# First FFN of a conditioned decoder layer: its first four hidden chunks computed from x*(1+scale), with the shift added afterwards as a bias, and eight conditioning blocks loaded in other stages

## The reference

```python
mod = silu(c) @ w_ada + b_ada              # (B, 9*1024)
sh1, sc1, gt1, sh2, sc2, gt2, sh3, sc3, gt3 = split(mod, 9)
h = x * (1 + sc1) + sh1
x = layer_norm(ALPHA * x + 0.5 * gt1 * swiglu(h, ffn1_w_in, ffn1_w_out))
h = x * (1 + sc2) + sh2
m = hybrid_mixer(h, ...)                   # conv branch and pooling branch, gated, one output projection
x = layer_norm(ALPHA * x + gt2 * m)
h = x * (1 + sc3) + sh3
x = layer_norm(ALPHA * x + 0.5 * gt3 * swiglu(h, ffn2_w_in, ffn2_w_out))
# swiglu: gate, up = split(h @ w_in, 2); (silu(gate) * up) @ w_out, hidden width 2816
```

## Time and profile before

| | |
|---|---|
| median of 3 runs | 1577.0 us |
| the profiled execution, its own time | 1571.29 us |
| its span on the slowest core (core 5) | 1569.7 us |
| spans of the 8 cores | 1556.7 to 1569.7 us |
| PE busy | 1479.4 us (94%), 9258 matmuls |
| PEld (weight loads, beside PE) | 856.3 us (55%) |
| DVE / ACT / POOL busy | 44% / 30% / 9% |
| chain of work that ended last | PE 84%, DMA 9%, DVE 3%, ACT 2%, issue 2% |
| DMA queue of POOL (q0), share of 16 engines | 48.6% |
| DMA queue of SP (q1), share of 16 engines | 20.9% |

### The profile page before, as it was taken

The page is one execution under the profiler, slowest core; times in us unless marked ns, Lnnn a source line. Parts: engine busy times, 40 slices in busy tenths (PEclk is TensorE's granted clock), DMA queues, the critical chain, the costliest instruction groups (busy, mean ns, idle before and its releaser), DMA issues.

```text
span 1569.7 us, 24460 instructions; the slowest of 8 cores (1556.7 to 1569.7 us)
## 1 busy us (share of the span) xinstructions
PE 1479.4 (94%) x9258; PEld 856.3 (55%) x9258; DVE 688.6 (44%) x935; ACT 472.9 (30%) x688; POOL 133.9 (9%) x253
## 2 busy tenths in 40 slices
PE   0799999999899999999999999999999999999995
PEld 0466666544344457765664564445666665444454
DVE  1223323565222465972377687237431134441255
ACT  0011112253112264672127456113531111421124
POOL 2011111000110000000000000000000010000000
PEclk9999999999999999999999999999999999999998
DMA  9989999869977868635386964457586465584522
GB/s 185 180 141 196 196 215 186 167 110 190 186 137 145 144 155 232 182 72 131 55 174 143 243 182 105 97 104 154 118 178 131 74 132 97 111 170 84 113 70 99
DMA packets 94980, 227.03 MB, mean 145 GB/s; under 512 B 10848, under 2 KB 36192, under 8 KB 94688
## 3 DMA queue, kind: packets, MB, share of 16 engines
q0 software_dynamic: 37136, 124.11, 48.6%
q1 hardware_dynamic: 57728, 101.36, 20.9%
HBM read 299.64 MB, written 40.11 MB: 216 GB/s over the span
## 4 chain that ended last, share of the span: by engine, by line
PE 84%; DMA 9%; DVE 3%; ACT 2%; issue 2%; SPq 0%; DVEq 0%; ACTq 0%; POOL 0%; POOLq 0%
PE ps L354 78%; PE ps L769 4%; DMA VS<-pool_w 3%; DMA ring<-ffn_w_in 2%; DMA VS<-R 2%; DMA XS<-tp_dr 1%; DMA ring<-w_ada 1%; DVE VB L322 1%; PE ps L418 1%; DVE hA L319 1%; ACT L315 1%; ACT scr L315 0%; PE ps L544 0%; ACT rstd_sb L315 0%; ACT VB L315 0%
## 5 line engine op out<-in xcount | busy, mean ns | idle before, releaser
L354 PE MATMUL ps<-hA,ring 128*128 128x348 bf16 x3072 | 467.2, 312 | 8.1 <-DMA ring<-ffn_w_in 3.6
L354 PE MATMUL ps<-hB,ring 128*128 128x512 bf16 x2048 | 450.9, 380 | 10.0 <-DVE mpv L513 5.3
L354 PE MATMUL ps<-R,ring 128*128 128x348 bf16 (+3 forms) x2378 | 398.7, 327 | 0.0
L354 PEld LDWEIGHTS ps<-hA,ring 128*128 128x128 bf16 x3072 | 298.1, 97 | 170.1 <-issue 9.6
L354 PEld LDWEIGHTS ps<-hB,ring 128*128 128x128 bf16 x2048 | 200.0, 98 | 250.6 <-issue 15.7
L315 ACT ACTIVATE scr<-ps 128x1044 f32<-128x1044 f32 (+1 forms) x136 | 140.3, 1032 | 633.8 <-PE ps L354 629.8
L354 PEld LDWEIGHTS ps<-R,ring 128*128 128x128 bf16 x2378 | 229.3, 97 | 163.1 <-issue 0.2
L319 DVE TENSOR_TENSOR R<-ps,scr 128x1024 bf16<-128x1024 f32 (+2 forms) x112 | 128.8, 1156 | 429.9 <-PE ps L354 387.0
L315 ACT ACTIVATE scr<-VB 128x1044 f32<-128x1044 f32 (+3 forms) x56 | 51.5, 919 | 296.8 <-DVE VB L322 121.1
L322 DVE SCALAR_TENSOR_TENSOR VB<-ps,modT,XS 128x1024 f32<-128x1024 f32 (+4 forms) x56 | 55.1, 983 | 97.1 <-PE ps L354 94.1
L303 POOL DMA_DIRECT2D ring<-ffn_w_in x88 | 46.6, 531 | 470.8 <-PE ps L354 440.2
(11 more groups left out here) (121 smaller groups left out, 802.7 us busy)
## 6 DMA issues: line engine op xcount, KB each, us to landing
ring<-ffn_w_in POOLq DMA_DIRECT2D x88, 512.0 KB, 10.0
ring<-w_in POOLq DMA_DIRECT2D x40, 512.0 KB, 7.5
ring<-w_ada POOLq DMA_DIRECT2D x36, 512.0 KB, 15.8
ring<-ffn_w_out POOLq DMA_DIRECT2D x48, 352.0 KB, 6.3
XS<-tp_dr SPq DMA_DIRECT2D x48, 288.0 KB, 4.5
tp_dr<-VS SPq DMA_DIRECT2D x32, 288.0 KB, 15.5
XS<-x_b SPq DMA_DIRECT2D x16, 512.0 KB, 9.8
VS<-R SPq DMA_DIRECT2D x128, 64.0 KB, 5.6
```

The lines of the kernel that those rows point to most:

```text
L354: ins = e.matmul(o, lt, rt[:, c0:c0 + n], start=(i == 0), stop=(i == nk - 1))
```

## The change

- In `setup` x of group A comes in three column tiles (1024 rows of 1392 B each) in place of four pairs of chunks, and only `ada_block(2)` and `(3)` are run, which now hold all of scale 1 (the host no longer reorders the columns). From each tile `hpre` = x*(1+scale) is made as soon as it is there, on VectorE (6 chunks) and ScalarE (2 chunks).
- `ffn_in_early` runs blocks 0 and 1 of the first FFN (j = 0 to 3) on `hpre`; block 0 tile by tile. The sums are copied from PSUM to eight spare places (`pre`).
- Then `ada_block(0)` and `(1)` (shift 1), `consts_early`, and `shift_bias`: 64 matmuls of 17 columns multiply the shift with the same weight blocks 0 and 1. `h_shifted` makes the usual `hA`, and the main loop starts at block 2. `finish_early` adds the bias to the saved sums in the hooks of j = 4 to 7.
- The ada blocks move: 4 to 8 at j = 6, 9, ..., 18; 9 to 11 at oc = 1, 3, 5 of the first FFN out of A; 12 to 15 in the mixer of A, after oc = 1, 3, 5, 7 of the second `gated` call; 16 and 17 in the mixer of B, after oc = 1 and 5 there.

```diff
@@ -419,8 +419,7 @@
                                        start=(k == 0), stop=(k == KC - 1))
                 return ins
             S.add("pe", fn, reads=[ring[:, s, :], cT[:, :, :]], writes=[ps[:, bank, 0:68]])
-            pieces = [(2 * i, 2, 0), (8 + 2 * i, 2, 34)] if i < 4 else [(4 * i, 4, 0)]
-            for idx, n, o in pieces:
+            for idx, n, o in [(4 * i, 4, 0)]:
                 src = ps[:, bank, o:o + n * 17].rearrange("p (m t) -> p m t", t=17)
                 dst = modT[:, idx:idx + n, :]
                 bb = baT[:, idx:idx + n].unsqueeze(2).to_broadcast([128, n, 17])
@@ -449,9 +448,10 @@
         def setup():
             dma("sp", "s_c", [(cin[:, :, :], c_all.rearrange("p (c t) -> p c t", t=17))], [], [cin[:, :, :]])
             dma("sp", "s_p", [(baT[:, :], ba_d[:, :]), (pT[:, :], pv_d[:, :])], [], [baT[:, :], pT[:, :]])
-            for i in range(4):
-                o = VB[:, 2 * i * GA.W:(2 * i + 2) * GA.W].rearrange("p (c n) -> p c n", c=2)
-                dma("sp", "s_x%d" % i, [(o, x_d["a"][2 * i:2 * i + 2].rearrange("c p n -> p c n"))], [], [o])
+            for i, (c0, n) in enumerate(GA.tiles):
+                o = XV[:, :, c0:c0 + n]
+                dma("sp", "s_x%d" % i, [(o, x_d["a"][:, :, c0:c0 + n].rearrange("c p n -> p c n"))], [],
+                    [chunk(VB, GA, c)[:, c0:c0 + n] for c in range(KC)])
             mset(ones_bf[:, :], 1.0 / D)
             mset(epsT[:, 0:1], EPS)
             mset(epsT[:, 1:2], EPS_DN)
@@ -460,11 +460,73 @@
             for m, f in gate_f.items():
                 b = baT[:, m * 8:(m + 1) * 8]
                 S.add("dve", lambda e, b=b, f=f: e.tensor_scalar_mul(out=b, in0=b, scalar1=f), reads=[b], writes=[b])
-            for i in range(4):
-                ada_block(i)
-                for c in (2 * i, 2 * i + 1):
-                    h_main(GA, c, chunk(VB, GA, c), 0, "dve")
-                    h_samp(GA, c, chunk(VB, GA, c), 0)
+            mset(hpre[:, :, NP + SW:GA.W], 0.0)
+            ada_block(2)
+            ada_block(3)
+            for c0, n in GA.tiles:
+                n = min(n, NP - c0)
+                for c in range(KC):
+                    o, i_ = hp(c)[:, c0:c0 + n], chunk(VB, GA, c)[:, c0:c0 + n]
+                    if c % 3 == 2:
+                        act(o, i_, AF.Identity, scale=modp(1, c))
+                    else:
+                        S.add("dve", lambda e, o=o, i_=i_, s=modp(1, c): e.tensor_scalar_mul(out=o, in0=i_, scalar1=s),
+                              reads=[i_, modp(1, c)], writes=[o])
+            xs_ = XV[:, :, NP:NP + SW]
+            tt(hpre[:, :, NP:NP + SW], xs_, modT[:, 8:16, 1:17], ALU.mult)
+
+        XV = VB[:, :].rearrange("p (c n) -> p c n", n=GA.W)
+        hpre = R[:, 14616:14616 + 8352].rearrange("p (c n) -> p c n", n=GA.W)
+        shb = cin[:, :, :].rearrange("p c t -> p (c t)").bitcast(BF16)[:, 0:KC * 17].rearrange("p (c t) -> p c t", t=17)
+        pre = [XS[:, i, :] for i in range(3)] + [mean_sb[:, :], rstd_sb[:, :]] + [
+            R[:, 8352 + 2088 * i:8352 + 2088 * i + 2088].bitcast(F32) for i in range(3)]
+
+        def hp(c):
+            return hpre[:, c, :]
+
+        def ffn_in_early(blk):
+            s = wblock(ffn_in_w[0][blk])
+            v = sl(s, KC, 512)
+            for jj in range(2):
+                j = 2 * blk + jj
+                groups = [[t] for t in range(GA.nt)] if blk == 0 else [list(range(GA.nt))]
+                for ts_ in groups:
+                    for b in range(2):
+                        o = b * 256 + jj * 128
+                        bk = bank(b, GA)
+                        mm([bk[t] for t in ts_], lambda k, o=o: v[:, k, o:o + 128], hp, KC)
+                act(P3(pre[2 * j], GA), pb(0, GA), AF.Copy)
+                cpy(P3(pre[2 * j + 1], GA), pb(1, GA))
+            return v
+
+        def shift_bias(vs):
+            cpy(shb, modT[:, 0:8, :])
+            for j in range(4):
+                for b in range(2):
+                    i = 2 * j + b
+                    o = b * 256 + (j % 2) * 128
+                    out = ps[:, 6, i * 17:(i + 1) * 17]
+                    mm([(out, 0, 17)], lambda k, o=o, j=j: vs[j // 2][:, k, o:o + 128], lambda k: shb[:, k, :], KC)
+            p6 = ps[:, 6, 0:136].rearrange("p (i t) -> p i t", t=17)
+            cpy(csb[:, :, :], p6[:, :, 1:17])
+            cpy(mpv[:, :, 0:1], p6[:, :, 0:1])
+
+        def h_shifted():
+            for c in range(KC):
+                h_main(GA, c, chunk(VB, GA, c), 0, "act" if c % 3 == 2 else "dve")
+            t = ctx[:, :, :]
+            tt(t, XV[:, :, NP:NP + SW], modT[:, 8:16, 1:17], ALU.mult)
+            tt(h_t["a"][:, :, NP:NP + SW], t, modT[:, 0:8, 1:17], ALU.add)
+
+        def finish_early(j):
+            a, b = pre[2 * j], pre[2 * j + 1]
+            for i, v in ((2 * j, a), (2 * j + 1, b)):
+                tt(v[:, NP:NP + SW], v[:, NP:NP + SW], csb[:, i, :], ALU.add)
+            z = scr[j % 2]
+            act(z[:, 0:NP], a[:, 0:NP], AF.Silu, bias=mpv[:, 2 * j, 0:1])
+            act(z[:, NP:GA.W], a[:, NP:GA.W], AF.Silu)
+            stt(hid(GA, j)[:, 0:NP], b[:, 0:NP], mpv[:, 2 * j + 1, 0:1], z[:, 0:NP], ALU.add, ALU.mult)
+            tt(hid(GA, j)[:, NP:GA.W], b[:, NP:GA.W], z[:, NP:GA.W], ALU.mult)
 
         def consts_early():
             dma("pool", "s_w", [(mask[:, :, :], mask_d.rearrange("p (c q) -> p c q", q=4)),
@@ -550,9 +612,9 @@
         def shift_state():
             dma("sp", "sshift", [(ncs_d[:, :, :], sconv[:, 1:30, :]), (nps_d[:, :, :], spool[:, 1:15, :])], [], [])
 
-        def ffn_in(g, f, hook):
+        def ffn_in(g, f, hook, b0=0):
             hh = h_t[g.name]
-            for blk in range(FC // 2):
+            for blk in range(b0, FC // 2):
                 s = wblock(ffn_in_w[f][blk])
                 v = sl(s, KC, 512)
                 for jj in range(2):
@@ -701,7 +763,7 @@
         def wpk(h):
             return ("wp_dr", 0, 1, 8 * h, 8 * h + 8)
 
-        def mixer(g, x1name, x1src):
+        def mixer(g, x1name, x1src, late_ada):
             first = g is GA
             hh = h_t[g.name]
             hrhs = lambda k: hh[:, k, :]
@@ -937,6 +999,8 @@
                         else:
                             stt(P3(z, g), P3(z, g), 1.0, pb(1, g), ALU.add, ALU.mult)
                             tt(merged(oc), z, m1, ALU.add)
+                            if oc % 2 and oc in late_ada:
+                                ada_block(late_ada[oc])
                         bg.step(2 if oc else 3)
 
             gated(8, lambda h: wblock(wp_dr[h], key=[wpk(h)]), pooled, UORD, True, gb_w)
@@ -1008,27 +1072,32 @@
         setup()
 
         def hook_f1in_a(j):
-            if j == 1:
-                consts_early()
-            if j >= 2 and j % 2 == 0 and j <= 12:
-                ada_block(4 + (j - 2) // 2)
-            if j in (15, 19):
-                ada_block(10 + (j - 15) // 4)
+            if j < 8:
+                finish_early(j - 4)
+            if j in (6, 9, 12, 15, 18):
+                ada_block(4 + (j - 6) // 3)
             if j >= 6:
                 build_toep(2 * (j - 6))
                 build_toep(2 * (j - 6) + 1)
             if j == 20:
                 consts_late()
 
-        ffn_in(GA, 0, hook_f1in_a)
+        v0 = ffn_in_early(0)
+        v1 = ffn_in_early(1)
+        ada_block(0)
+        ada_block(1)
+        consts_early()
+        shift_bias([v0, v1])
+        h_shifted()
+        ffn_in(GA, 0, hook_f1in_a, 2)
         h0b = gen_h0b()
 
         def hook_f1out_a(oc):
             next(h0b, None)
             if oc == 0:
                 next(h0b, None)
-            if oc in (1, 4):
-                ada_block(12 + oc // 4)
+            if oc in (1, 3, 5):
+                ada_block(9 + oc // 2)
 
         ffn_out(GA, 0, 2, lambda oc: chunk(VB, GA, oc), hook_f1out_a)
         scv = sample_loads(sconvT, 480)
@@ -1042,8 +1111,6 @@
             if j == 8:
                 spl.append(sample_loads(spoolT, 240))
                 fold_loads()
-            if j in (4, 9, 14, 19):
-                ada_block(14 + (j - 4) // 5)
             if j == 12:
                 fold_scale()
             if 13 <= j < 21:
@@ -1070,9 +1137,9 @@
 
         ffn_out(GB, 0, 2, feeder(feed), hook_f1out_b, mid_f1out_b)
         bg.add(gen_ln(GB, "ln1_g", "ln1_b", 3, xr_d["b", 1], "xr1b"))
-        mixer(GA, "xr1a", xr_d["a", 1])
+        mixer(GA, "xr1a", xr_d["a", 1], {1: 12, 3: 13, 5: 14, 7: 15})
         bg.add(gen_ln(GA, "ln2_g", "ln2_b", 6, xr_d["a", 2], "xr2a"))
-        mixer(GB, "xr1b", xr_d["b", 1])
+        mixer(GB, "xr1b", xr_d["b", 1], {1: 16, 5: 17})
         dma("sp", "o_s", [(gls_d[:, :], gls[:, :, :].rearrange("p c s -> p (c s)")),
                           (ups_d[:, :], ups[:, :, :].rearrange("p c s -> p (c s)")),
                           (ncp_d[:, :], ncp_sb[:, :, :, :].rearrange("p c q m -> p (c q m)")),
```

6 lines of the change are left out of this document (removed).

## The result

The changed kernel takes 1623.35 us in the median, the kernel before 1577.03: a ratio of 1.0268, 95% interval 1.0232 to 1.0305, slower. Run again in a later series (`e0_again`) the changed kernel gave a ratio of 1.0293 (1.0238 to 1.0348). I had forecast 1603.5 with 1611 as the upper end: the direction was right, the size was short by 20 us (16 by 1619.2). The profiled execution took 1625.56 us, 54.3 more than the profiled one of before; that pair lies 8 us further apart than the medians, because the one of before was 5.7 us under its median and this one is 2.2 over.

The account below looks back on a forecast made before the run. DMA delivery was taken to set the pace of the start, PE to bound the rest; start 23.4, `pool_w` -2.3 and mixer of A 5.6 sum to 26.7 us, so 1603.5 us, range 1590 to 1611.

Parts of the forecast that it names:

- the 32 matmuls ahead: Start: PE runs tiles 0 and 1 of j = 0, 32 matmuls at 0.149 us each, before the last x tile.
- the landing of FFN block 2: Behind `shift_bias`: POOL issues at 3.4 us after j = 3, first half lands 5.4 us later, PE starts at 9.7.
- the term for the mixer of A: Ring loads w7, co1 and o0 come late in the mixer of A: +5.6 us (0 to 18).
- the mixer of B: One ada block per half, w7's slot free early, co1 in time: nothing, up to 2 us if late.
- when x comes: Start: the two DMA queues alternate row by row, so x tiles are used at about 42, 57 and 64 us.
- rival 1: Start: x tiles get a larger share of the engines, last tile at 53 us, total 1592.5 us; chance 0.11.
- `mpv`: First FFN in of B: `pool_w` lands in time, no wait near 400 us, -2.3 us (0 to -7.2).
- the clock behind long waits: PE's granted clock falls to 0.50 after a wait of 4 us or more, costing 1.9 us each time.
- a sign of being wrong: Mixer of A: ring waits of 1 to 2 us each; missing or over 3 us each, the forecast is wrong.
- none for 1.5 us: PE loses no time to a lowered clock after a wait of 1.5 us.
- Rival 2: Mixer of A: late blocks, each gap takes the clock down, three times 1.9 us; 12.7 us more, 1616; chance 0.07.
- Rival 3: All cores: relieved DMA queues gain up to 13 us, faster if x is complete before 48 us; chance 0.05.

Follow-up runs that it names:

- e0_again: The changed kernel itself, unaltered, run again in a later series: 1622.54 us, ratio 1.0293 to the kernel before.
- e4_x_rows: Kernel before with only x of group A loaded in three column tiles instead of four pairs of chunks: 1596.4 us, ratio 1.0157.
- e6_x_first: `e1_sample_order` with POOL held at the second FFN block until the last x tile has landed: 1596.0 us, ratio 1.0119 to the kernel before.
- e1_sample_order: Changed kernel with the sample-column product of hpre written behind the matmuls of tiles 0 and 1: 1608.5 us, ratio 1.0241 to the kernel before.
- e3_moves_alone: Kernel before with its own start, only the ada blocks moved as in the change: 1590.02 us, ratio 1.0118.
- e5_hold_w_in: Changed kernel with the mixer of B's first two w_in blocks held until chunk 4 of the output projection is summed: 1613.1 us, ratio 1.0263.
- e10_best: Changed kernel, sample product later, POOL held until x tile 1, ada 0/1 beside ring, h_shifted before j = 3, ada 12-17 in first FFN in of B: 1566.3 us.
- e9_h_on_act: Changed kernel with all 8 chunks of h_shifted on ScalarE instead of 6 on VectorE: 1614.92 us, ratio 1.0276 to the kernel before.

## Why the prediction was right in direction and wrong in size

Four steps failed: the 32 matmuls ahead, the landing of FFN block 2, the size of the term for the mixer of A, and the mixer of B, which was put at nothing.

**Right: when x comes.** Tiles at 42, 57 and 64 us were forecast; 39.3, 58.5 and 62.4 were measured, from "they alternate row by row, whatever a row carries". `e4_x_rows` shows the turn by itself, `e6_x_first` what it costs (21 us for the last tile). The Trainium skill, "DMA: Bandwidth & Descriptors", section "Queues, rings and completion order", has an engine drain a packet of many descriptors from a queue before it turns to the next. As a larger share for x, which is what the prediction made of it in rival 1, the rule is not borne out: 959 rows passed beside 962, and here the measurement decides (packets of equally many rows from both queues would show the same counts, so the rows speak against the larger share, not against packets). Rival 1 is refuted: its last tile would have come at 53 us.

**Right: `mpv`, the clock behind long waits, the place of the wait for block 2.** The wait for `mpv` is gone from every core, and the -2.3 us for it is what the mean of the cores gives. Behind the gap of 8.3 us the granted clock was again 0.50 and the loss 2.4 us (forecast 1.9):

```profile
109.00:110.00 1.00, 0.29 (x2) 0.19 (x3) 0.00 (x0) 0.00 (x0) 0.00 (x0) 0.50 1.05 139
```

**Wrong: "The tile order gains only what PE does ahead: tiles 0 and 1 of j = 0, 32 matmuls."** It gained one matmul. I had used the very fact for `hA` ("the sample columns of all chunks are written last and every chain reads them") and not asked it of `hpre`, which is written in the same way. `e1_sample_order` shows it. From the last tile to the end of j = 3 it took 34.1 us, not 28.1: 4.6 for 31 of the 32 matmuls, 0.4 for `hpre` of the last tile (2.5 us, not 2.1), and the rest in the clock and the waits for the copies out of PSUM, which no row separates.

**Wrong in size: "issues at 3.4, and the first half lands 5.4 us later at the earliest".** POOL issued at 4.7: the last copy out of PSUM and the bias additions on VectorE put `shift_bias` at +3.1 and not +2.5, and the issue came 1.6 us behind its start, not 0.9. The first use came 8.5 us behind it. The 5.4 of the earlier trace rows is the minimum of many landings, and I took it for the usual one: this half block landed in 5.5 to 8.0 us, by core. PE began block 2 at +13.2, not +9.7. `h_shifted` ended at 107.4, 2.3 us before: on core 2 the DMA decided, not VectorE. Where the half landed in 5.5 to 5.7 us VectorE did, 6.4 us after the issue; its end, +10.9 on core 2, was put at +9.6.

The start by terms, on core 2: last tile -1.8 (64.2 before rounding), to the end of j = 3 +6.0, to block 2 +3.5, clock +0.5. Together +8.2 on the 23.4 forecast, 31.6.

**Wrong in size and with a step missing: "Mixer of A: ... +5.6 us", "Mixer of B: ... nothing".** In the mixer of A the places were right: w7, co1 and o0, one wait for each half. They cost 9.8 us there (8.4 in `e3_moves_alone`), and one of them, 3.60 us, is over the 3 us that I had set as a sign of being wrong. The first half of w7 was used 6.8 us after the issue at 773.18 and its second half 12.4 us after it, where I had 5.4 and 8.6; the longest wait, 3.6 us, is for that second half. The missing step is what stands behind: the ada blocks free their slots at once, so POOL no longer waits between `w_out` and the `w_in` of the next mixer, and the ring's rows take turns with the feed of x. VectorE comes late and PE waits 7.7 to 8.4 us, counting the same waits behind the mixer of B. I had followed the slots up to o1 and stopped. `e5_hold_w_in` shows this link behind the mixer of A. With -2.3 for `pool_w` these waits come to 9.2 + 7.7 - 2.3 = 14.6 of the 18.5 us of `e3_moves_alone`, whose interval is 14.6 to 22.5.

**Where the 53 us stand.** How many us longer each stage takes than in the kernel before, by the start of the same matmuls on PE, in the mean of the eight cores of a profiled execution, with 0.81 us counted off or on for each ada block that has moved:

| | forecast | changed | `e0_again` | `e3_moves_alone` |
|---|---|---|---|---|
| start (to the first FFN out of A) | 23.4 | 29.4 | 29.5 | -0.3 |
| first FFN in of B | -2.3 | -2.3 | -2.3 | -2.3 |
| mixer of A with its output projection | 5.6 | 14.6 | 15.7 | 13.2 |
| mixer of B with its output projection | 0 | 10.3 | 6.3 | 7.9 |
| rest | 0 | 1.1 | 0.8 | 0.9 |
| end | 26.7 | 53.1 | 50.0 | 19.4 |

The mixer of B, which I had put at nothing, costs 6 to 10 us. Of these 3.5 are the waits for `VB` on core 2 and 0.7 the one for co1; the cores also wait there for `ts` (4.9 us on core 2, 1.2 on core 5 of before) and `cwv<-tp_dr` (4.1 and 0.9), which differ much from core to core. What makes the rest stays open.

**Not so in general: "none for 1.5 us", on the clock.** PE on core 2 of `e3_moves_alone`, and a stretch of 1 us behind that wait:

```profile
786.55 2.83 PE L354 MATMUL ps<-R,ring 128*128 128x348 bf16 x12 [1.52 <-DMA ring<-w_out]
...
788.00:789.00 1.00, 1.00 (x5) 0.46 (x3) 0.00 (x0) 0.00 (x0) 0.00 (x0) 0.50 0.99 131
```

Behind a wait of 1.52 us for o0, with an ada block in front of it, the granted clock fell to 0.50, and 12 matmuls took 2.83 us in place of 1.94; behind the same wait of 1.19 us on core 2 of the changed kernel it stayed at 1.00. The rows of the prediction had a wait of 5.3 us with the loss and one of 1.45 without, and nothing between.

**The rivals.** Rival 2 (waits breed waits, 1616) came nearest in number, but mostly by another way: on core 2 of the changed kernel the gaps in the mixer of A stayed under 2 us but for one, and the matmuls behind them ran at full speed. The clock did add to it elsewhere: behind the wait of 4.9 us for `ts` in the mixer of B 80 matmuls took 18.94 us, in the kernel before 17.43. Rival 3 is refuted: L was 62.4, and in `e3_moves_alone`, with less load in the early stages and the old start, the fastest core took 1577.9 us, longer than the slowest of before (1569.7). `e10_best` is faster by its start, not by this relief.

## What to carry to other kernels

When two queues are busy, count rows and not bytes: the same x in three times the rows was complete at 67.2 us and not at 49.1 (`e4_x_rows`), and holding the other queue brought its last tile from 62.4 to 41.3 (`e6_x_first`). When a tile is written in parts so that a consumer can begin early, check every writer of that buffer, the small strided one above all, since its region may span all of it. When a load is taken out of or put into a ring, follow the slots to the next stage too: a slot that comes free early starts a transfer that can collide with whatever feeds the engines there, as `w_in` did with `xr1a`. For the time from issue to landing take the range over several cores, not the minimum on one.

## What was not expected of the hardware

- One and the same half block, the first of four issued behind each other, lands in 5.5 to 8.0 us depending on the core, and the second in 8.1 to 10.8; the cores of `e9_h_on_act` (5.3 to 7.3 for the first) and `e0_again` (5.6 to 7.7) spread in the same way.
- POOL takes 0.68 us to issue a DMA while VectorE makes `hA` (2.72 us for 4), 0.55 when ScalarE makes it (2.18 for 4, `e9_h_on_act`). The landings did not come earlier by it.
- A row of x (1392 B) costs an engine about 3.5 us x 16 x 0.914 / 887 = 0.058 us when nothing else runs (145 of the 887 are constants under 512 B); the prediction's 0.085 was high. Since a turn is 0.40 us of weights and this, it hardly showed: 62.4 us against 64.
